# Two attention orders made one: scores ahead of transposes on TensorE, the maximum ahead of the copy of turned columns on DVE

## What is computed

```
s = einsum(q, k) * scale          # + bias or mask in the windowed kinds
p = softmax(s)                    # exp(s - max(s)) / sum
o = einsum(p, v)
```

## Time and profile before

| | us |
|---|---|
| median of 3 runs | 4858.56 (4851.97 to 4868.57) |
| the profiled execution | 4862.26, of which the span 4860.6 |
| PE busy | 3743.6 (77%) |
| DVE busy | 2448.4 (50%) |
| ACT busy | 2216.2 (46%) |
| POOL busy | 913.2 (19%) |
| mean granted clock of TensorE | 0.889 |

### The profile page before, as it was taken

One profiled execution on the slowest core, in us unless ns is written; L12 is line 12 of the kernel. 1 busy time (PEld: TensorE's weight loads), 2 busy tenths in 40 slices (PEclk: granted clock), 3 DMA queues, 4 the chain that ended last, 5 costly groups with the idle time before them and its releaser, 6 DMA issues. The chain is left out here.

```text
span 4860.6 us, 70948 instructions
## 1 busy us (share of the span) xinstructions
PE 3743.6 (77%) x24823; PEld 3029.3 (62%) x24823; DVE 2448.4 (50%) x4502; ACT 2216.2 (46%) x3911; POOL 913.2 (19%) x749
## 2 busy tenths in 40 slices
PE   3986786877459999278988869675778997879557
PEld 3974565656348888266766657554656775658446
DVE  2114453442477888475425545455575425546454
ACT  1215454651047777322226657554432226657442
POOL 0213000000026665043540000000034440000002
PEclk7998898988679999689999989887889998989878
DMA  6227413303879999322323242422232223232423
GB/s 218 100 108 224 97 37 77 106 31 131 274 270 391 398 393 345 115 88 83 103 80 70 77 87 57 87 84 76 80 101 67 98 93 76 78 77 58 104 81 94
DMA packets 328087, 634.15 MB, mean 130 GB/s; under 512 B 115048, under 2 KB 171272, under 8 KB 326696
## 3 DMA queue, kind: packets, MB, share of 16 engines
q1 hardware_dynamic: 292436, 510.46, 33.4%
q0 software_dynamic: 33840, 113.66, 7.3%
q10 hardware_dynamic: 1444, 5.30, 0.3%
HBM read 490.39 MB, written 138.95 MB: 129 GB/s over the span
## 5 line engine op out<-in xcount | busy, mean ns | idle before, releaser
L1882 PE MATMUL pr_ps<-pr_wH,hT_part 128*128 128x512 f32 x1120 | 445.6, 398 | 0.0
L1652 ACT ACTIVATE ex_high<-ex_ring 128x2048 fp32r<-128x2048 f32 x192 | 368.6, 1920 | 98.0 <-PE ex_pg L1628 39.6
L1698 DVE TENSOR_TENSOR ex_ring_part<-ex_ring,ex_high 128x2048 fp32r<-128x2048 f32 x144 | 372.4, 2586 | 51.3 <-ACTq L1653 39.6
L1882 PE MATMUL pr_ps<-pr_wH,x_sb_part 128*128 128x512 f32 x896 | 363.9, 406 | 22.5 <-DVEq L1955 22.5
L1882 PE MATMUL pr_ps<-pr_w_part,x_sb_part 128*128 128x512 f32 x896 | 356.6, 398 | 0.0
L1144 DVE TENSOR_REDUCE aa_nm<-aa_ps 128x1 f32<-128x1280 f32 (+1 forms) x144 | 197.7, 1373 | 305.7 <-PE aa_ps L1045 304.9
L1593 POOL TENSOR_TENSOR ex_ring_part<-ex_ring,ex_high 128x2048 fp32r<-128x2048 f32 x48 | 239.3, 4985 | 216.5 <-ACTq L1653 216.5
L1055 PE MATMUL aa_ps<-ident,aa_prob 128*128 128x128 f32 x1312 | 209.0, 292 | 61.8 <-ACTq L1181 60.1
L1177 ACT ACTIVATE aa_prob<-aa_ps,aa_nm 128x512 f32<-128x512 f32 (+2 forms) x272 | 211.1, 776 | 87.9 <-DVEq L1145 44.4
L1144 DVE TENSOR_REDUCE ab_nm<-ab_ps 128x1 f32<-128x1280 f32 (+1 forms) x108 | 148.3, 1373 | 194.7 <-PE ab_ps L1045 194.4
L1882 PEld LDWEIGHTS pr_ps<-pr_wH,hT_part 128*128 128x128 f32 x1120 | 216.5, 193 | 47.1
(11 more groups left out here) (356 smaller groups left out, 9203.6 us busy)
## 6 DMA issues: line engine op xcount, KB each, us to landing
ex_ring<-in_w_gate SPq DMA_DIRECT2D x64, 1024.0 KB, 9.6
ex_ring<-in_w_up SPq DMA_DIRECT2D x64, 1024.0 KB, 8.2
ex_ring<-in_w_down SPq DMA_DIRECT2D x64, 1024.0 KB, 7.9
z_d<-pr_zT POOLq DMA_DIRECT2D x120, 256.0 KB, 3.0
rt_mw<-in_w_ada SPq DMA_DIRECT2D x14, 2048.0 KB, 16.0
pr_w<-in_w_in SPq DMA_DIRECT2D x14, 2048.0 KB, 9.0
mod_w<-in_w_ada SPq DMA_DIRECT2D x10, 2048.0 KB, 13.2
proj<-pr_raw POOLq DMA_DIRECT2D x60, 256.0 KB, 2.3
```

The costliest lines, as they stand in the source:

```text
L1652: scalar.activation(wH[:, c % HL].bitcast(F32R), w_sb[:, c % SL], ACT.Copy)
L1698: vector.tensor_tensor(w_part[:, c % SL].bitcast(F32R), w_sb[:, c % SL], wH[:, c % HL], ALU.subtract)
L1882: mm = tensor.matmul(ps[:, g % 4, :], x.bitcast(F32R), w[:, c % 2, kk, :].bitcast(F32R), start=kk == 0 and i == 0, stop=kk == KC - 1 and i ...
```

## The change

The case `LAG == 2` loses its own order on PE and on DVE. In all stages PE now runs `scores(h)` ahead of `transposes(h - LAG)`, and DVE runs the division, the maximum of `h` and then `turned_part(h - LAG)`. ACT, SP and POOL are as before, and so are all waits, credits and operations; nothing is added or removed. Stages with `LAG == 1` come out as they were.

```diff
                     for h in range(n + 4 + LAG):
                         g = h - LAG
-                        if h < n and LAG == 1:
+                        if h < n:
                             scores(h)
                         if 0 <= g < n:
                             transposes(g)
-                        if h < n and LAG == 2:
-                            scores(h)
                         if g % 2 == 0 and g >= 4:
                             turned((g - 4) // 2)
...
                     for h in range(n + 4 + LAG):
                         g = h - LAG
-                        if LAG == 2:
-                            turned_part(g)
                         if g % 2 and g >= 5:
                             m = (g - 5) // 2
...
                             dve.drain().then_inc(mx, 1)
-                        if LAG == 1:
-                            turned_part(g)
+                        turned_part(g)
                 iterate(dve, body)
```

## The result

The kernel after takes 4808.59 us (median of 4 runs, 4804.65 to 4817.29) against 4858.31 us for the kernel before in 4 runs on the same chip: a ratio of 0.9898, with a 95% interval from 0.9876 to 0.9920. The gain is 49.7 us; the forecast was 4817, or 41 us. The profiled execution of the kernel after took 4807.27 us, its span is 4805.6, and the mean granted clock is 0.893 against 0.889.

What follows compares the result with a forecast made beforehand. No engine is full; a ring of waits through several engines sets the pace. Shorter rings give -3 (`am`), -10 (`ad`) and -28 (`ac`), -41 us, so 4817 against the median of 4858.6; range for 8 in 10: 4797 to 4838.

Steps and rivals of the forecast that it cites:

- forecast's 6.21: Stage `ac`: DVE becomes the ring, a pair takes 6.21 us against 6.85, a change of -0.64.
- the 28 us: Both `ac` stages: summed gain, counting 22 of 24 near-tile pairs in each layer and nothing for the context pairs.
- Rival B: Stage `ac`: splitting PE's longest idle raises the clock, saving another 17 us, -58 in all, 4800 us; chance 0.15.
- 7.88: Stage `am`: pair time on the new ring over scores, maximum and copy, against 7.98; -3 us over 28 pairs.
- 6.72: Stage `ad`: pair time on the new ring through ACT, against 7.09; -10 us over 28 pairs.
- gap of the kind that the forecast named: Stage `ad`: possible gap between scores and transposes, 0 to 0.17 us a step, at most 10 us, none taken.
- The unknown handover: From a copy's end to the next scores in the changed stages: taken as 0.14 us, allowed up to 0.34.
- Rival A: Late credit costs more: handover 0.34 makes `am` 8.28 and `ac` 6.41 a pair; -21 us, 4838; chance 0.11.
- Rival C: Clock falls in `am` and `ad`, kernel gets slower: at 0.75, +29 us, 4888; chance 0.04.
- argument against C from `ab`: Stage `ab` already has the new order, waits 0.75 us before its scores and keeps clock 1.00 over 180 us.
- Rival D: Stage `ac`: scores wait for ACT's copy, pair stays at 6.85, only 13 us gained, 4846; chance 0.05.
- What would show it: Signs in `am`, `ad`, `ac`: pairs 7.9, 6.7, 6.2 us; PE idle 0.7 or more before scores in `am` and `ac`.

Runs made afterwards that it cites:

- e4_before_twice: Kernel before, with every pass of the scores in the two `ac` stages run twice, results unchanged: 4859.5 us, ratio 0.9997.
- e6: Kernel after, with the reciprocal of DVE's division run a second time, and a drain, in `am` and `ad`: 4808.18 us, ratio 0.9893.
- e10: Kernel after measured and profiled once more, with no edit: 4809.84 us, ratio 0.9898.
- e2_dve_only: Kernel after, but PE keeps transposes ahead of scores for LAG 2, so only DVE's order is changed: 4832.52 us, ratio 0.9944.
- e1_pe_only: Kernel before, with only PE's order changed (scores ahead of transposes everywhere), DVE's old order kept: 4986.45 us, ratio 1.0258.
- e8: Kernel after, with ACT copying all turned columns in `am` and `ac` and DVE none: 4757.06 us, ratio 0.9787.

## Why the prediction was right, and where it wasn't

The direction and the mechanism held: shorter rings, no work removed, the gain in the four stages with `LAG == 2` and most of it in `ac`. The sum came to 41 of the measured 49.7 us (53.1 by the stages of the profiles): `ac` gave 10 us more than forecast and `am` 4 more, `ad` 2 less.

- *`ac`: right ring, right pair, too small a sum.* The forecast's 6.21 was measured as 6.22, with its terms each in its row: maximum to copy 1.41, copy to the next maximum over the division 1.77 for 1.78, the copy 0.42, the handover 0.15 for 0.14, scores to maximum 1.04 for 1.05. What the 28 us left out are the clock (3.7 and 2.9 us by e4_before_twice), and that the gain is not 0.64 in every pair: pairs of the edge tiles with 256 near keys went from 6.61 and 6.51 at full clock (last `ac` of e4) to 5.73 and 5.85 (that of e6), and I took 22 pairs of 24 and none of the context pairs. By e4 ring and clock give 16.0 + 3.7 and 15.2 + 2.9.
- *Rival B (0.15) happened in part.* The clock rose from 0.84 and 0.86 to 0.92 and 0.95, and it came with the splitting of PE's idle that B named; but it brought some 7 to 8 us by the two estimates at e4, not 17. The forecast and B weren't exclusive, and I had priced them as if they were.
- *`am`: 7.73 instead of 7.88.* The mis-sized term is maximum to copy, 1.41 from the earlier trace rows. That row's copy carries a wait of 0.19 for the transposes; without it the term is 1.34. With 1.68 for 1.70 and 0.15 for 0.14 the step is 3.86. The pairs then gave much more than the 3 us: summed from first to last turned output of each iteration, the stage is 13.6 us shorter, since the drain is shorter too (the 13th and 14th pair 7.96 and 6.02 before, 6.69 and 3.80 after). What ate 6 us of it is the fill, for which the forecast had no term: 23.19 us instead of 20.40 at the stage's start, and 29.90 instead of 26.58 between the iterations (23.56 and 28.97 in e10). Part of that is the third step's scores ahead of the first transposes (first scores to first transposes 6.69 and 7.16 us instead of 5.28). But it isn't all: e2_dve_only has only two steps' scores there (5.11 and 5.10 us) and fills no faster, 23.32 and 29.58. Its scores, and after them those of the kernel before:

```profile
512.57 1.62 PE L1045 MATMUL am_ps<-am_kT,am_qT 96*128 96x512 f32 x6
...
516.43 1.63 PE L1045 MATMUL am_ps<-am_kT,am_qT 96*128 96x512 f32 x6 [1.37 <-DVEq L1113]
...
520.30 1.60 PE L1045 MATMUL am_ps<-am_kT,am_qT 96*128 96x512 f32 x6 [1.37 <-DVEq L1113]
```

```profile
512.71 1.64 PE L1045 MATMUL am_ps<-am_kT,am_qT 96*128 96x512 f32 x6
...
515.55 1.65 PE L1045 MATMUL am_ps<-am_kT,am_qT 96*128 96x512 f32 x6
...
518.10 1.65 PE L1045 MATMUL am_ps<-am_kT,am_qT 96*128 96x512 f32 x6
```

  With DVE's new order the ring of the forecast holds from the first steps on, 3.86 us a step. The old order starts these scores 2.84 and 2.55 us apart, as long as no values and no division stand on its ring. So the new ring is the shorter one only in the steady part. That drain (some 7 us) and fill (some 6) nearly cancel is luck: neither is in the forecast's sum.
- *`ad`: 6.87 instead of 6.72.* One piece of the ring was mis-sized; the others are 3.52, 0.80 and 1.25 for 3.53, 0.81 and 1.25. The 1.13 from transposes to the copy behind them is 1.30 (847.75 to 849.05): the eight weight loads that stand right behind scores take 1.02 us and not 0.85, because the first of them starts while the last scores' matmul still runs, 0.23 us ahead of its own matmul. This is a gap of the kind that the forecast named and took at nought (0 to 0.17 a step). Of the gain of 7.9 in the table less seems due to the order: over the profiles of all kernels here the stage takes 249.4, 244.2, 244.4 and 245.9 under the old order and 237.5 to 243.7 under the new, with means of 246.0 and 240.4. That is 5.6 us, about 26 pairs of 0.22, with a scatter as large as itself.
- *The unknown handover.* 0.14 and 0.15 us, though PE passes two waits. That the earlier trace rows gave it was luck in part: the row of the weight load there names ACT's credit as what ended the wait (L1167), and both copies ended within 0.01 us of each other, so it could not tell the one handover from the other. Rival A fell: no pair shows more, and in `am` the late credit still leaves a shorter ring.
- *Rival C (0.04) was wrong for the change and right as a mechanism.* In the kernel after the clock of the steady stretches of `am` and `ad` is 1.00. In e1_pe_only, where the idle at the turned output is 2.10 us and more, it is 0.92 in a steady stretch of `am` and 0.77 and 0.73 in `ac`, and the kernel is 126 us slower. The Trainium skill's rule that frequent short idles between groups swing the clock ("TensorE: Matmul & The Clock Gate", section "A second HAM failure mode: psum-queue depth-cycling") was put as the argument for C: the waits that the new ring of `am` adds (0.34 us in the row above) didn't do it, those of e1 did. The forecast's argument against C from `ab` was weak: in those 180 us PE's matmuls cover 172.8, and it stands idle before its scores only six times (0.54 to 1.21 us).
- *Rival D fell.* In `ac` the scores wait for DVE (L1111), not for ACT. It is e8, with DVE's copy gone, where ACT holds them, at 5.32 and not 6.85.
- *What would show it.* Most signs came: 0.2 from maximum to copy is 0.12 in `am` (541.09 + 1.22 to 542.43), PE's waits of 0.7 and 1.2 us before the scores in `ac`, ACT's wait in `ac` under 1, `aa` and `ab` unmoved. One failed: in `am` PE waits 0.34 and 0.24 us before the scores, not 0.7 and more. One didn't come in full: in `ac` scores are released by DVE's copy in both steps of a pair; in one of them nobody waits for that.

The forecast's own upper bound of 4832 doesn't follow from its terms: 4817, the gap of 10 and half of A's 21 give 4837. The measured time lies inside either.

What stays open: why the second `ac` keeps a clock of 0.88 with PE's old order and DVE's new (e2_dve_only, 9.1 us) where the first doesn't, what else makes up the 24 us between that kernel and the kernel after, and some 2 us of the span outside the four stages.

## What to carry to other kernels

Where no engine is full, write the ring of waits down term by term, both the one that goes and the one that the late credit makes; here this gave pair times to 0.01 us in `ac` and to 0.15 in the other two stages, where a term was taken from a row with a wait in it (`am`) or with other work ahead of it (`ad`). The ring of the steady part isn't that of the fill and the drain; in `am` these moved by 6 and 7 us. Orders on two engines have to be judged together (PE's alone cost 126 us, DVE's alone gave 28, both gave 50): where DVE copies, moving scores ahead on PE pays only if DVE's reduction no longer waits for the copy behind it. And ask which engine on the ring could hand its piece to one that waits: giving DVE's copies to ACT brought another 51.5 us.

## What the hardware showed that I had not expected

- *PE's spare work can be free and even useful.* Doubling the scores of `ac` in the old order raised the clock of the two stages from 0.84 and 0.86 to 0.97 and 0.96 and made them 3.7 and 2.9 us shorter in the profile; the whole kernel's ratio is 0.9997 [0.9988, 1.0007]. As a means to lift the clock it was worth no more than that.
- *Weight loads for transposes depend on what stands ahead.* Eight of them take 0.85 and 0.86 us after values and 1.02 to 1.03 after scores. The single load takes 0.14 us in both; behind scores the first one starts early and the second follows after 0.23 us instead of 0.06.
- *More idles of PE alone don't lower the clock.* In `am` after, PE waits before the scores of every step (0.34 and 0.24 us) and keeps 1.00, and its idle time in 68 us is less than before (4.9 against 7.6 us); with 2.10 us and more at each turned output (e1) it has 0.92. Whether the length of one idle decides or their sum (68.00 - 63.10 = 4.9 us of a stretch against 68.00 - 52.83 = 15.2) these runs don't tell apart.
- *A first step at the lower clock.* After 33 us without work, six scores of `am` took about 2.7 us (5.49 for twelve) instead of 1.61, so a third step's scores ahead of the first transposes put these 1.4 to 1.9 us later at each fill of `am` (6.69 and 7.16 us after the first scores instead of 5.28).
